# Neighbourhood attention in pairs of heads over bands of 128 keys, with tokens in column order and the masked bias table built early in DRAM

## The reference

```python
s = jnp.einsum('bjqhd,brjchd->bhjqrc', q_blk, k_band) * scale
s = s + jnp.transpose(bias, (0, 2, 3, 1, 4))[None]
s = jnp.where(col_mask[None, None, :, :, None, :], s, MASK_VALUE)
prob = jax.nn.softmax(s.reshape(s.shape[:4] + (kh * COL_BAND,)), axis=-1)
o = jnp.einsum('bjqrc,brjchd->bjqhd', ...)
```

## Time and profile before

| | us |
|---|---|
| median of 3 runs | 847.31 (847.02 to 848.36) |
| the profiled execution | 845.59 |
| its span, first to last instruction | 843.9 |
| TensorE busy | 769.8 (91%) |
| VectorE busy | 434.9 (52%) |
| ScalarE busy | 282.0 (33%) |
| GpSimd busy | 147.3 (17%) |
| mean granted TensorE clock | 0.971 |

### The profile page before, as it was taken

One profiled execution on the slowest core, in us unless ns is written; L12 is line 12 of the kernel. 1 busy time (PEld: TensorE's weight loads), 2 busy tenths in 40 slices (PEclk: granted clock), 3 DMA queues, 4 the chain that ended last, 5 costly groups with the idle time before them and its releaser, 6 DMA issues.

```text
span 843.9 us, 10686 instructions
## 1 busy us (share of the span) xinstructions
PE 769.8 (91%) x3993; PEld 413.7 (49%) x3993; DVE 434.9 (52%) x963; ACT 282.0 (33%) x527; POOL 147.3 (17%) x140
## 2 busy tenths in 40 slices
PE   3777889999999999899999898998999999999897
PEld 3655735534434433347887754455343443334365
DVE  6999543544334333326868886426433433423264
ACT  5161144522222221126756353334312212211163
POOL 5696500000000000002077624000000000000000
PEclk9899979899999999999999997999999999999999
DMA  6052195799999999996578490364999999999911
GB/s 225 1 158 101 33 422 206 286 358 421 421 421 422 421 423 421 421 400 214 200 178 302 150 262 7 150 249 199 340 418 421 421 421 421 422 421 420 406 67 50
DMA packets 60429, 246.83 MB, mean 292 GB/s; under 512 B 14566, under 2 KB 15672, under 8 KB 37464
## 3 DMA queue, kind: packets, MB, share of 16 engines
q1 hardware_dynamic: 58280, 241.66, 72.8%
q0 software_dynamic: 2096, 4.45, 2.6%
HBM read 244.48 MB, written 1.61 MB: 292 GB/s over the span
## 4 chain that ended last, share of the span: by engine, by line
PE 73%; DVE 10%; POOL 7%; issue 6%; ACT 2%; DMA 1%; SPq 0%; DVEq 0%; ACTq 0%
PE PS L1903 27%; PE PS L1931 14%; PE PS L1941 7%; PE PS L1691 7%; PE PS L1858 4%; PE PS L2177 3%; PE PS L1813 2%; PE PS L1873 2%; PE PS L2150 1%; PE PS L1914 1%; POOL bias_a L699 1%; PE PS L1789 1%; POOL bias_b L699 1%; POOL qrs L710 1%; POOL s5W L641 1%
## 5 line engine op out<-in xcount | busy, mean ns | idle before, releaser
L1903 PE MATMUL PS<-ring,xw 128*64 128x512 f32 x1024 | 230.9, 604 | 14.6 <-issue 12.2
L1903 PEld LDWEIGHTS PS<-ring,xw 128*64 128x64 f32 x1024 | 79.1, 139 | 161.9 <-issue 161.3
L1931 PE MATMUL PS<-ring,actT 128*64 128x512 f32 x512 | 116.9, 598 | 1.2 <-DVE actT L1411 0.6
L605 POOL TENSOR_TENSOR rstd<-ms,mhalf 128x2 f32<-128x2 f32 x6 | 4.3, 712 | 570.2 <-DVE ms L1087 564.0
L1411 DVE COPY actT<-PS 128x256 f32<-128x256 f32 x32 | 13.5, 423 | 172.0 <-PE PS L1914 172.0
L926 ACT ACTIVATE ohi<-PS 128x512 fp32r<-128x512 f32 x64 | 38.2, 597 | 144.3 <-PE PS L1931 144.3
L1425 DVE TENSOR_TENSOR olo<-PS,ohi 128x512 fp32r<-128x512 f32 x64 | 44.2, 691 | 81.8 <-ACT ohi L926 81.6
L918 ACT ACTIVATE act<-PS,wslot 128x256 f32<-128x256 f32 x32 | 15.2, 474 | 177.2 <-PE PS L1903 177.2
L1394 DVE SCALAR_TENSOR_TENSOR act<-rows,pid 128x256 f32<-128x256 f32 x128 | 61.8, 483 | 14.1 <-DMA rows<-rows_d 10.7
L1691 PE MATMUL PS<-ringr,hTh 128*128 128x512 f32 x160 | 63.4, 396 | 4.8 <-DVE ringr L1112 3.1
L1112 DVE SCALAR_TENSOR_TENSOR ringr<-ring,gcol,dwh 128x512 fp32r<-128x512 f32 x80 | 60.5, 810 | 12.7 <-ACT dwh L783 12.0
(11 more groups left out here) (334 smaller groups left out, 1047.1 us busy)
## 6 DMA issues: line engine op xcount, KB each, us to landing
ring<-in_moe_w_down SPq DMA_DIRECT2D x64, 1024.0 KB, 22.4
ring<-in_moe_w_gate SPq DMA_DIRECT2D x56, 1024.0 KB
ring<-in_moe_w_up SPq DMA_DIRECT2D x56, 1024.0 KB
ring<-in_nat_w_qkv SPq DMA_DIRECT2D x6, 2048.0 KB
ring<-in_ple_w_gate SPq DMA_DIRECT2D x4, 2048.0 KB
ring<-in_s_w_out SPq DMA_DIRECT2D x2, 2048.0 KB
ring<-in_moe_w_gate SPq DMA_DIRECT2D x16, 256.0 KB, 6.8
ring<-in_moe_w_up SPq DMA_DIRECT2D x16, 256.0 KB, 7.6
```

What stands on the lines that cost most here:

```text
L1903: ins = mm(PS[CAP * h_:CAP * h_ + CAP, 0, :].rearrange("p (u f) -> p u f", u=2), xw[:, p % 2, k, CAP * h_:CAP * h_ + CAP], wv[h_][:, k], s ...
L1931: ins = mm(PS[CAP * h_:CAP * h_ + CAP, 2 + n, :], actT[:, k, CAP * h_:CAP * h_ + CAP], wd[h_][:, k, 512 * n:512 * n + 512], start=k == 0, ...
```

## The change

Tokens stand in column order: partition p of tile `t` is the token of row `p % 4` and column `32t + p // 4`. `x`, `p` and the output are loaded and stored so by the access pattern (`tokens`). The S5 mixer keeps the old order; the permutation is made when the first norm's transposes are evicted (`by_row`) and when the GELU output is written.

In this order a block of 16 query columns is 64 partitions, and its band of 32 columns x 4 rows is 128 neighbouring keys. Scores are taken for a pair of heads at once: 4 blocks x 2 heads, each a matmul of 64 x 64 weights and 128 columns. The probabilities of a pair are 4 x 128 per query instead of 2 x 2 x 256. Values of blocks 1 and 2 begin inside a tile; copies of them (`vb`) are made by 8 DMAs of GpSimd.

The bias table is made in DRAM (`bias_d`, 2 MB) with the mask in it: first filled with -1e30 from an SBUF tile (`blank`), then 124 DMAs from DRAM to DRAM write the windows (`windows_set`), 64 of them with one window of 16 elements for each of 8, 16, 16 or 9 columns and 16 heads, 60 with windows that are clipped at the grid's edge. They stand on the SP queue. Later GpSimd loads the whole table with one DMA. The 32 loads and 16 mask additions on GpSimd go. The first pair's scores, bias and exponentials are put ahead of the last chunk of the projection and of the last eviction.

```diff
+def tokens(ap, t):
+    (step, _), rest = list(ap.ap[0]), [list(d) for d in ap.ap[1:]]
+    return bass.AP(ap.tensor, ap.offset + BAND * t * step, [[step, BAND], [GW * step, ROWS]] + rest)
...
+        def by_row(ap):
+            return ap.rearrange("p k (r t c) -> p k t c r", r=ROWS, t=TT)
...
@@ sync
+            def windows_set():
...
+                for j in range(4):
+                    t, s_ = divmod(j, 2)
+                    base_ = 64 * s_ * row_n + t * KB
+                    c0, c1 = ((8, QB), (0, QB), (0, QB), (0, 9))[j]
+                    k0 = QB * j - WC // 2 - BAND_AT[j]
+                    for rq in range(ROWS):
+                        for rk in range(ROWS):
+                            dst = bass.AP(bias_d.tensor, base_ + (ROWS * c0 + rq) * row_n + rk * BAND + c0 + k0,
+                                          [[ROWS * row_n + 1, c1 - c0], [TT * KB, NH], [1, WC]])
+                            src = bass.AP(rpb.tensor, (rk - rq + WR - 1) * R + WC // 2 - 1,
+                                          [[0, c1 - c0], [H, NH], [1, WC]])
+                            sp.dma_start(dst, src).then_inc(S("windows_set"), 16)
+                        for c in (range(c0) if j == 0 else range(c1, QB)):
...
+                            sp.dma_start(dst, src).then_inc(S("windows_set"), 16)
...
+            sp.wait_ge(S("blank_ready"), 1)
+            sp.dma_start(bias_d.rearrange("p (a n) -> p a n", n=512), bc(blank[:, :], 1, NH * TT * KB // 512))\
+                .then_inc(S("bias_blank"), 16)
             sp.wait_ge(S("uT_half"), 2)
...
             load(IT["w_out"][1])
+            sp.wait_ge(S("bias_blank"), 16)
+            windows_set()
             sp.wait_ge(S("y_done"), 2)
...
@@ gpsimd
-            bias_load(0)
-            qk_pow(0)
-            qk_pow(1)
-            bias_mask(0, 0, 2)
-            qk_pow(2)
-            bias_mask(0, 2, 7)
-            qk_pow(3)
-            bias_mask(0, 7, 8)
+            pool.wait_ge(S("windows_set"), 16 * WINDOWS)
+            pool.dma_start(bias[:, :, :, :, :].rearrange("p h t r c -> p (h t r c)"), bias_d)\
+                .then_inc(S("bias_loaded"), 16)
+            for w in range(4):
+                qk_pow(w)
             pool.wait_ge(S("qk_T"), 8)
-            bias_load(1)
-            bias_mask(1, 0, 8)
...
@@ vector
+            def scores(i):
...
+                tt(prob[:, b].rearrange("p (h t) (c r) -> p h t c r", h=2, c=BAND),
+                   PS[:, b0:b0 + 2, 0:256].rearrange("p h (t c r) -> p h t c r", t=TT, c=BAND),
+                   bias[:, 2 * i:2 * i + 2].rearrange("p h t r c -> p h t c r"), ALU.add).then_inc(S("sb_ready"), 1)
...
+                tt(prob[:, b], prob[:, b], bc(rr[:, b, :], 2, KB), ALU.mult).then_inc(S("prob_ready"), 1)
...
@@ tensor
+                for j in range(4):
+                    t, s_ = divmod(j, 2)
+                    k0 = ROWS * BAND_AT[j]
+                    for h_ in range(2):
+                        r = slice(64 * h_, 64 * h_ + 64)
+                        ins = mm(PS[64 * s_:64 * s_ + 64, SB[i % 2] + h_, KB * t:KB * t + KB], qT[r, i, 64 * j:64 * j + 64],
+                                 kT[r, i, k0:k0 + KB], start=True, stop=True)
...
+                for j, v_ in enumerate((vt[:, 0], vb[:, 0], vb[:, 1], vt[:, 1])):
+                    for h_ in range(2):
+                        a = 2 * i + h_
+                        ins = mm(PS[64 * h_:64 * h_ + 64, 4 + i % 2, 64 * j:64 * j + 64], v_[:, HD * a:HD * a + HD],
+                                 probT[:, i % 2, TT * h_ + j // 2, 64 * (j % 2):64 * (j % 2) + 64], start=True, stop=True)
```

More of the change, by code:

```diff
@@ L39 @@
 WR, WC = 8, 16
+QB, BAND = 16, 32
+KB = BAND * ROWS
+BAND_AT = (0, 8, 24, 32)
+HPAIRS = NH // 2
 MASKV = -1e30
@@ L430, in load @@
                 for j, (c, src) in enumerate(parts):
-                    w = 1
-                    for m in src.shape[1:]:
-                        w *= m
+                    w = math.prod(src.shape) // P
                     dst = ring[s][:, c:c + w]
-                    if len(src.shape) == 3:
+                    if len(src.shape) == 3 and src.shape[0] == P:
                         dst = dst.rearrange("p (k n) -> p k n", k=src.shape[1])
@@ L472, in _ @@
                     .then_inc(S("b_loaded"), 16)
[L473 removed]
+            for t in range(TT):
+                sp.dma_start(x[:, t, :], tokens(I["x"][0], t)).then_inc(S("x_loaded"), 16)
             sp.dma_start(gain_s[:, :], bc(gains[0], 0, P)).then_inc(S("gain_s_loaded"), 16)
@@ L689, in _ @@
                         .then_inc(S("qkw_loaded"), 16)
[L691 to L706, removed]
             def qk_pow(w):
@@ L1625, in _, with out_evict @@
+            def out_evict(i):
+                ve.wait_ge(S("pv_done"), i + 1)
+                ve.tensor_copy(oT[:, i, :], PS[:, 4 + i % 2, 0:T]).then_inc(S("oT_ready"), 1)
+            for i in range(HPAIRS + 3):
+                if i < HPAIRS:
+                    scores(i)
+                if i == 1:
+                    qkv_evict(5)
+                if 1 <= i <= HPAIRS:
+                    normalise(i - 1)
+                if i >= 3:
+                    out_evict(i - 3)
             for n in range(4):
@@ L2143, in values @@
-            def values(a):
-                pe.wait_ge(S("probT_ready"), a + 1)
-                if a >= 4 and a % 2 == 0:
-                    pe.wait_ge(S("oT_ready"), a // 2 - 1)
-                r = slice(64 * (a % 2), 64 * (a % 2) + 64)
-                for kt in range(2):
-                    ins = mm(PS[r, 4 + (a // 2) % 2, 0:T], vt[:, kt, HD * a:HD * a + HD], probT[:, a % 2, kt, :],
-                             start=kt == 0, stop=kt == 1)
-                ins.then_inc(S("pv_done"), 1)
@@ L2154, in _ @@
-            for a in range(NH + 3):
-                if a < NH:
-                    scores(a)
-                if a == 2:
-                    keep_busy(2, 5)
-                if 2 <= a < NH + 2:
-                    prob_T(a - 2)
-                if a >= 3:
-                    values(a - 3)
-            pe.wait_ge(S("oT_ready"), NH // 2)
+                    if (w, c) == (5, 2):
+                        scores(0)
+            scores(1)
+            keep_busy(2, 5)
+            for i in range(2, HPAIRS + 3):
+                if i < HPAIRS:
+                    scores(i)
+                if i < HPAIRS + 2:
+                    prob_T(i - 2)
+                if i >= 3:
+                    values(i - 3)
```

214 lines of the change are left out of this document (104 added, 110 removed).

## The result

The changed kernel takes 858.13 us (median of 4 runs, 856.1 to 860.46) against 847.43 (847.02 to 848.36) for the kernel before, measured beside it: a ratio of 1.0126 [1.009, 1.0161], slower by 10.7 us, where 840 was forecast. The profiled execution is the one of 856.1 us; its span is 854.4, TensorE is busy for 746.5 us of it (before 769.8) at a mean granted clock of 0.953 (before 0.971). TensorE does less work and waits more.

A forecast was written before the change was run, and what follows sets the result against it. The weight-load stream was taken to bound the expert stage, VectorE the changed attention. Profiled 845.59 - 25.3 (attention) - 1.5 (masks) + 1.3 (token order) + 18 (late loads) = 838.1, as a median 840 us; range 822 to 864.

The forecast's parts named there:

- the price of one issue: Load queue: each of the 124 writes takes 0.504 us to issue, 62.5 in all, so the queue is free at 134.8.
- rival 1: Load queue: DMA engines can't write windows as fast as issued, from 49 ns a packet; slower overall from 55; chance 0.23.
- The mechanism behind it: Expert stage: late queue delays weights, routing rows and second pair (189.5 instead of 173.0), so the stage ends 18 us later.
- Each us by which the 124 come later adds one: Load queue: every further us of delay in the 124 writes adds one us to the 18 us loss.
- the bend: Load queue: no loss is left if the 124 writes are through by 117 us, 0.36 us each.
- its term: Attention stage: pairs of heads over 128 keys save 25.3 us, output projection starting at 514.8 instead of 540.1.
- Rival 2: Load queue: the table is hidden after all, issues at 0.36 us or less or gaps absorbing delay; 822 us; chance 0.12.
- Rival 3: Attention: TensorE becomes the bound at 4.7 us a pair instead of 3.2, giving 851 us; chance 0.15.
- Two tiles sharing: Attention on TensorE: two small score matmuls share the array, so a pair's scores take 0.85 us.
- Attention and the masks: Attention and projection: -25.3 us from pairs of heads and -1.5 from masks and table loads leaving GpSimd.
- the 0.2 for handovers: Attention on VectorE: 0.2 us for handovers within the 3.2 us a pair.
- The cost of token order: Stepped first eviction (+0.8 us) and x loaded in two DMAs (+0.5): +1.3 us, between 0 and 3.

The follow-up runs named there:

- e2: The kernel before with the same 124 table writes put on its load queue, into a tensor nothing reads: 887.3 us, ratio 1.0507.
- e4: The changed kernel with only the 64 full windows, the 60 clipped writes left out: 819.33 us, ratio 0.9711 to the kernel before.
- e9: The kernel without table writes, plus eight groups of 8 small probe DMAs after its output; one execution: 0.47 to 1.46 us an issue.
- e3: The changed kernel with the table written by 31 DMAs after 4 that gather its rows, bias addition split in two: 819.47 us, ratio 0.9689 to before.
- e8: The kernel before without mask additions and without the second table load: 835.73 us, ratio 0.9896.
- e1: The changed kernel without the 124 window writes, the table holding only -1e30: 817.0 us, ratio 0.9676 to the kernel before.
- e7: The changed kernel with the 124 writes spread, ten behind each expert pair's loads from the fifth on: 850.95 us, ratio 1.0048 to the kernel before.

## Why the prediction was wrong

**The step that failed is the price of one issue.** "One issue costs: the eight small loads of `us`, the nearest in shape (three dimensions, short rows), take 4.03 us, 0.504 each". In their place the runs show 0.694 in the changed kernel, 0.699 in e2 (71.78 to 158.44), 0.758 in e4. The row was near in shape (three dimensions, short rows) and far in what matters: one of its ends is in SBUF, both ends of a window are in DRAM. e9 puts that at 0.47 against 0.64 to 0.67 with the rest alike. The 0.04 to 0.11 between the probe's window (0.65) and the kernels is unexplained. 124 x 0.19 = 23.6 us (the writes began 1.4 us earlier than reckoned, so 22.1 came), and the highest price that I considered was 0.6 (free at 146.7), though nothing in the rows excluded more. The point from which the whole change turns slower stood in rival 1, free at 142, but tied to another mechanism. That 858 lies within the range of 822 to 864 is no merit: the top of the range was drawn for rival 1, and the forecast had the other side of the kernel before.

**The mechanism behind it held in each step that the runs can check.** Three pairs of weights from when the queue is free, then the routing rows, the second pair, and the end of the stage with it. "Each us by which the 124 come later adds one": 18 + 22.1 makes 40.1; measured are 39.5 at the second pair and 41.5 at the stage's end. Pairs late in the stage are 14.99 apart, where 14.9 was named as the sign. The second pair's matmuls start 3.5 us after the rows have landed (208.96 to 212.49), as taken. e3 (first load at 106.67) lies before the bend and loses nothing that can be told, e4 (119.49) just behind it. With 0.694 in the sum the forecast is 838.1 + 22.1 = 860.2; less the 4.8 that attention gave beyond its term, 855.4, for a profiled run of 856.1.

**Rival 1 gave the right sign for the wrong reason.** The DMA share is 0.09 to 0.32 while the windows are written, where this rival needs one near 1.00. The trace of the changed kernel has a record of each of the 16,384 packets of 64 bytes: they took 11 ns in the mean, so 14 us on the busiest engine with its 1264, in 86 us of issues, and far below the 49 ns from which they would decide. The Trainium skill's rule ("DMA: Bandwidth & Descriptors", Specifications) on writes below 512 bytes may cost something within those 11 ns; it decides nothing here. Rival 2 was excluded by the 86 us, yet e3 is its result reached by another way. Rival 3 came only for a stretch, and not at its price of 4.7 us a pair: with TensorE at the lower clock and without a gap a pair took 3.15 (532.88 to 536.03), and at the higher one TensorE waits. From start to start the scores took 1.07 us at a granted clock of 0.50 (536.03 to 537.10), 0.54 at the full one. Two tiles sharing would need 0.85 and four 0.43 to 0.45, so more than two of the four share the array, where I had taken two.

**Attention and the masks gave more: 31.6 instead of 26.8.** From the second pair's scores (524.02) to the output projection (550.02) it took 26.0 us, where 28.1 were worked out. From start to start the add takes 1.10 (537.23 to 538.33) and maximum and reciprocal 0.80, as worked out (1.09 and 0.79); the multiplication takes 0.61 and the copy 0.33, where the durations of the rows, 0.69 and 0.42, count the overlap of neighbours twice, and the 0.2 for handovers was not there. Where TensorE set the pace, the pair took the 3.16 that I had for VectorE (3.2), which is chance. From the stage's end to the scores it took 105.1 instead of 108.5, so 3.9 us went there with the new first scores (0.6) counted, not 1.5; e8 gives 2.4 of it to the masks. The cost of token order, 1.3, can't be seen: in e1 the second pair starts 2.2 us earlier than in the kernel before.

## What to carry to other kernels

Before moving small DMAs onto the queue that feeds the bound, multiply their number by the price of one issue of the same kind (which memory its ends are in, as well as its shape), and hold it against the cover; if no row has the kind, the range must reach well past the nearest. Then merge before looking for a better place: 35 issues instead of 124 turned +1.3% into -3.1%, while moving the 124 behind loads that were the bound gave +0.5%. And a long wait in the chain (25.6 us here) is worth only what the next bound behind it allows: removing it gave 4 to 5.

## What the runs showed of the hardware

- With nothing else under way, an issue on the load queue took 0.62 to 0.67 us with both ends in DRAM and 0.47 with one in SBUF, the same for 16 and for 256 rows, and 1.46 for 1024 rows of 64 bytes (e9, one execution). In the kernels the table's writes took 0.69 to 0.76 in the mean, and 256 rows cut as 4 x 64 took 0.88 (e3).
- Between weight loads under way, issues of the same small writes took 1.0 to 1.7 us in the mean of ten, single ones over 4 (e7).
- A packet of 64 bytes from DRAM to DRAM took 11 ns of a DMA engine (16,384 records in the changed kernel), and 12 between weight loads (e7).
- A small write issued behind three pairs' weights (18 MB, part of them still to come) on the same queue landed 25.6 us after its issue (changed kernel). With none under way (DMA share 0.02 from 163.4 to 164.9) the load behind it was issued 1.45 us after it (kernel before).
- Sixteen float32 records of 128 columns on 64 x 64 tiles take 0.67 us, and 1.07 from start to start at half the clock: more than two tiles at once.
